# Value rows of tile 0 summed by VectorE, those of the other tiles in fours of slots, and a tenth ring place

## The reference

```
z   = x @ w_in                                   # q, k, v, GLU value, GLU gate
att = dilated sliding-window attention(q, k, v)  # 8 heads of 64
cv  = swish(LayerNorm(causal depthwise conv of the GLU output, 31 taps))
x1  = LayerNorm(ALPHA * x + concat(att, cv) @ w_out)
# PEER: 8 heads, each picks 16 of 16384 experts for each position
q   = x1 @ w_query
top 16 of both halves of the keys, then the best 16 of the 256 sums -> experts, gates
y_p = sum over the 128 chosen experts e:  gate_e * gelu(x1 . U[e]) * V[e]
y   = LayerNorm(ALPHA * x1 + y_p)
```

## Time and profile before

| | us |
|---|---|
| median of 3 runs (lowest to highest) | 4052.86 (4046.16 to 4052.99) |
| profiled execution | 4054.08 |
| its span | 4052.3 |
| VectorE busy | 2703.9 (67%) |
| TensorE matmuls busy | 2865.7 (71%) |
| GpSimd busy | 1203.4 (30%) |
| ScalarE busy | 682.6 (17%) |
| bytes moved by DMA | 1385.80 MB, mean 342 GB/s |

### The profile page before, as it was taken

The page is one execution under the profiler, slowest core; times in us unless marked ns, Lnnn a source line. Parts: engine busy times, 40 slices in busy tenths (PEclk is TensorE's granted clock), DMA queues, the critical chain, the costliest instruction groups (busy, mean ns, idle before and its releaser), DMA issues.

```text
span 4052.3 us, 41343 instructions
## 1 busy us (share of the span) xinstructions
PE 2865.7 (71%) x14768; PEld 1255.5 (31%) x14768; DVE 2703.9 (67%) x7412; ACT 682.6 (17%) x1484; POOL 1203.4 (30%) x1092
## 2 busy tenths in 40 slices
PE   6976554778567667666766876687677666779766
PEld 5422221334222313332332333233223332223311
DVE  4233343335586998699679868976997696445965
ACT  1200012210022013102310330132014101121000
POOL 0011111111144433433444344424333442223232
PEclk8987777889788888888888888879878988889989
DMA  9954468577689998998999899979988999999888
GB/s 334 345 202 155 151 225 290 206 277 291 226 328 408 411 366 326 422 413 345 372 419 400 330 395 419 394 290 416 414 355 325 421 408 391 415 417 365 335 329 349
DMA packets 217518, 1385.80 MB, mean 342 GB/s; under 512 B 27416, under 2 KB 38168, under 8 KB 66648
## 3 DMA queue, kind: packets, MB, share of 16 engines
q0 software_dynamic: 156672, 1140.92, 70.6%
q1 hardware_dynamic: 40384, 142.88, 9.8%
q10 hardware_dynamic: 20256, 99.35, 6.4%
HBM read 1369.94 MB, written 80.04 MB: 358 GB/s over the span
## 4 chain that ended last, share of the span: by engine, by line
PE 33%; DMA 29%; DVE 25%; issue 10%; POOL 2%; ACT 1%; DVEq 0%; ACTq 0%; POOLq 0%; SPq 0%
DMA t<-in_expert_uv,t 28%; PE psum L1367 20%; DVE t L1036 8%; PE psum L1214 4%; DVE t L1047 3%; PE psum L1256 2%; PE psum L1234 2%; POOL t L603 2%; DVE t L984 1%; DVE t L982 1%; DVE t L985 1%; DVE t L983 1%; PE psum L1245 1%; DVE t L927 1%; DVE t L981 1%
## 5 line engine op out<-in xcount | busy, mean ns | idle before, releaser
L1367 PE MATMUL psum<-t,t 64*64 64x512 f32 x5696 | 1627.2, 712 | 777.9 <-DVE t L1047 777.6
L603 POOL DMA_INDIRECT t<-in_expert_uv,t x1088 | 1203.2, 1106 | 2819.4 <-PE psum L1367 1403.2
L1036 DVE CUSTOM_DVE_ANT_0 t<-t,t 128x1024 f32<-128x1024 f32 x1088 | 1325.2, 1222 | 1039.0 <-DMA t<-in_expert_uv,t 1031.5
L1367 PEld LDWEIGHTS psum<-t,t 64*64 64x64 f32 x5696 | 415.9, 155 | 1746.1 <-DVE t L1047 983.1
L1363 PE MATMUL psum<-t,t 64*64 64x512 f32 x2496 | 760.4, 738 | 0.0
L754 ACT ACTIVATE t<-t 128x2 f32<-128x2 f32 x544 | 110.6, 203 | 2472.5 <-DVE t L1036 2465.6
L1047 DVE TENSOR_SCALAR t<-t,t,t 128x64 f32<-128x64 f32 x1088 | 294.0, 321 | 68.0 <-ACT t L754 59.1
L1324 PEld LDWEIGHTS psum<-t,t 128*128 128x128 f32 x2304 | 271.7, 197 | 54.0 <-issue 53.9
L1324 PE MATMUL psum<-t,t 128*128 128x128 f32 (+1 forms) x2304 | 281.8, 282 | 0.0
L1214 PE MATMUL psum<-t,t 128*128 128x128 f32 (+2 forms) x768 | 253.8, 489 | 8.2 <-DMA t<-in_xT 7.5
L903 DVE SCALAR_TENSOR_TENSOR t<-t,t,t 128x128 f32<-128x128 f32 x840 | 237.8, 344 | 0.0
(11 more groups left out here) (132 smaller groups left out, 1965.4 us busy)
## 6 DMA issues: line engine op xcount, KB each, us to landing
t<-in_wq_t ACTq DMA_DIRECT2D x63, 1024.0 KB
out<-in_cache_k_win SPq DMA_DIRECT2D x8, 4080.0 KB
out<-in_cache_v_win SPq DMA_DIRECT2D x8, 4080.0 KB
t<-in_w_in_t ACTq DMA_DIRECT2D x44, 512.0 KB, 5.1
t<-in_kc_t SPq DMA_DIRECT2D x8, 2560.0 KB
t<-in_vc_t SPq DMA_DIRECT2D x8, 2560.0 KB, 13.7
t<-in_expert_uv,t POOLq DMA_INDIRECT x1088
t<-in_w_v_t ACTq DMA_DIRECT2D x6, 1024.0 KB, 8.6
```

What stands on the lines that cost most here:

```text
L603: pool.indirect_dma_start(ring[:, r, :], None, I["expert_uv"], bass.IndirectOffsetOnAxis(ap=idn[t % 2][:, s:s + 1], axis=0)).then_inc(land ...
L1036: dve.tensor_tensor_reduce(out=ring[:, r, 0:D], in0=x1[t % 2][:, :], in1=ring[:, r, 0:D], scale=1.0, scalar=0.0, op0=ALU.mult, op1=ALU.add ...
L1367: last = pe.matmul(MAIN[t][half][NS * a:NS * a + NS, :], zt[NS * a:NS * a + NS, k % Z_RING, j, :], vv[NS * a:NS * a + NS, :], start=(p == ...
```

## The change

- Tile 0: no matmuls. `first_values` (DVE) multiplies two coefficients by their gates and then adds each V row, scaled, into two PSUM banks, one instruction of 128x1024 a slot. The new semaphore `v_done` counts them and releases ring places one at a time.
- Tiles 1 to 8: `gelu`, `weigh` and `values_quad` work on four slots. `weigh` is now two instructions: a product of four columns and one 128x256 product with both operands broadcast. `pv` counts fours. The lag of DVE and PE is one place, and DVE does the dot of a place before it weighs. `AUX_QUADS` are slots 12 to 119 (before 16 to 119).
- `RING` is 10; `wq0` and its load go, and every tile loads head 0's weights with head 1's.
- 48 early slots in place of 49, with gates of three heads in place of four.
- The 31 taps spread over 40 places, and `conv_rows` to `ln1_end` and `x1_transposes` come three to eight places later (the transposes of the attention keep theirs); the two output projections are two places apart in place of four, both `ln1_half` one place apart; `queries` and `query_copy` come two and one places later.

```diff
-RING, FIRST_RING = 9, 4
-Z_RING = 3
+RING, FIRST_RING = 10, 4
+Z_RING = 2
+TAP_SPAN = 40
-EARLY = ROUTE_STEP
-EARLY_GATES = (EARLY * (PH - 1) + TOP - 1) // TOP
+EARLY = 3 * TOP
+EARLY_GATES = EARLY // TOP
-AUX_PAIRS = range(8, PAIRS - 4)
+AUX_QUADS = range(3, QUADS - 2)
+def batch(t):
+    return 4 if t else 2
+            if (_s + 1) % batch(_t) == 0:
+                BATCH_PLACE.setdefault(place(_n, _q), []).append((_t, _s // batch(_t)))
+def tap_at(q):
+    return range(q * CK // TAP_SPAN, (q + 1) * CK // TAP_SPAN) if q < TAP_SPAN else range(0)
-        wq0 = at(o_l, [P, KD, 2 * KEYC])
-        zt = small([P, Z_RING, 2, NS])
+        zt = small([P, Z_RING, 4, NS])
+        first_sum = psum[:, 6 * 512:8 * 512]
-            sp.dma_start(wq0[:, :, :], I["wq_t"][0]).then_inc(wq0_in, 16)
...
# gather (POOL)
-                        pool.wait_ge(pv, pair(0, s - FIRST_RING) + 1)
+                        pool.wait_ge(v_done, s - FIRST_RING + 1)
-                        pool.wait_ge(pv, pair(1, k - RING) + 1)
+                        pool.wait_ge(pv, (k - RING) // 4 + 1)
# route_loads, query_copy (ACT)
-                for h in (1, 2):
+                for h in (0, 1):
-                if 1 <= h < PH - 2:
+                if h < PH - 2:
# DVE
-            def weigh(t, p):
-                k = PAIRS * t + p
-                dve.wait_ge(a_gelu, k + 1)
+            def weigh(t, c):
+                k = quad(t, c)
+                d4, g4 = dots[t % 2][:, 4 * c:4 * c + 4], gtn[t % 2][:, 4 * c:4 * c + 4]
+                dve.wait_ge(a_gelu, gelus(t, c) + 1)
+                step(dve.tensor_tensor(d4, d4, g4, ALU.mult))
                 if k >= Z_RING:
                     dve.wait_ge(pv, k - Z_RING + 1)
-                for j in range(2):
-                    s = 2 * p + j
-                    dve.tensor_scalar(zt[:, k % Z_RING, j, :], ident2[:, :], dots[t % 2][:, s:s + 1], gtn[t % 2][:, s:s + 1],
-                                      ALU.mult, ALU.mult).then_inc(zt_ready, 1)
+                dve.tensor_tensor(zt[:, k % Z_RING, :, :], ident2[:, :].unsqueeze(1).broadcast_to([P, 4, NS]),
+                                  d4.unsqueeze(2).broadcast_to([P, 4, NS]), ALU.mult).then_inc(zt_ready, 1)
+            def first_values(c):
+                d2 = dots[0][:, 2 * c:2 * c + 2]
+                dve.wait_ge(a_gelu, gelus(0, c) + 1)
+                step(dve.tensor_tensor(d2, d2, gtn[0][:, 2 * c:2 * c + 2], ALU.mult))
+                for s in (2 * c, 2 * c + 1):
+                    r, _ = spot(0, s)
+                    w_ = dots[0][:, s:s + 1]
+                    if s == 0:
+                        dve.tensor_scalar(first_sum, ring[:, r, D:ROW], w_, None, ALU.mult).then_inc(v_done, 1)
+                    else:
+                        dve.wait_ge(v_done, s)
+                        dve.scalar_tensor_tensor(first_sum, ring[:, r, D:ROW], w_, first_sum, ALU.mult, ALU.add).then_inc(v_done, 1)
-                        for t, p in pairs_at(n, q, 2):
-                            weigh(t, p)
                         for s in slots_at(n, q):
                             dot(max(n, 0), s)
+                        for t, c in batches_at(n, q, 1):
+                            if t:
+                                weigh(t, c)
+                            else:
+                                first_values(c)
-                if m and 4 * g + i < CK:
-                    taps(m, 4 * g + i)
+                for k in tap_at(4 * g + i) if m else ():
+                    taps(m, k)
-                if g in (12, 13) and i == 2:
-                    ln1_half(m, g - 12)
+                if g == 14 and i in (0, 1):
+                    ln1_half(m, i)
# PE
-                pe.wait_ge(zt_ready, 2 * (k + 1))
-                for half in range(2):
-                    for j in range(2):
+                pe.wait_ge(zt_ready, k + 1)
+                for two in range(2):
+                    for half in range(2):
+                        for j in (2 * two, 2 * two + 1):
-                if g in (11, 12):
-                    out_projection(m, g - 11)
+                if g == 13 and i in (1, 3):
+                    out_projection(m, i // 2)
-                        for t, p in pairs_at(n, 4 * g + i, 3):
-                            values_pair(t, p)
+                        for t, c in batches_at(n, 4 * g + i, 1):
+                            if t:
+                                values_quad(t, c)
```

More of the change, by code:

```diff
@@ L820, in front @@
                     weights_T(m, g - 1)
+                for h in range(PH):
+                    if g == QUERY_AT[h] and i == 3:
+                        query_copy(m, h)
+                        if h == 0:
+                            x1_rows(m)
                 if i != 2:
                     return
-                if g == 9:
+                if g == 11:
                     conv_std(m)
-                if g == 10:
+                if g == 12:
                     conv_swish(m)
@@ L844, in _ @@
                     for i in range(4):
-                        for t, p in pairs_at(n, 4 * g + i, 0):
-                            gelu(t, p)
+                        for t, c in batches_at(n, 4 * g + i, 0):
+                            gelu(t, c)
                         if m < PT:
@@ L1315, in queries @@
                     pe.wait_ge(x1T_ready, KD * (m + 1))
[L1317 to L1321, removed]
+                pe.wait_ge(wq_in[h % 2], 16 * (4 * m + h // 2 + 1))
+                w_ = wq[:, h % 2, :, :]
                 for side in range(2):
@@ L1339, in key_scores, with values_quad @@
                 last.then_inc(a_s, 1)
[L1341 to L1345, removed]
+            def values_quad(t, c):
+                k = quad(t, c)
+                w = slots(t) // 4
+                aux = t in AUX_TILES and c in AUX_QUADS
+                if c == 0:
                     if t == 1:
@@ L1351, in values_pair @@
                         pe.wait_ge(satt_T, 2 * NB)
[L1352 removed]
+                if aux and c == AUX_QUADS.start:
                     pe.wait_ge(res_done, t)
[L1354 to L1368 removed]
@@ new lines, in values_quad @@
+                pe.wait_ge(zt_ready, k + 1)
+                for two in range(2):
+                    for half in range(2):
+                        for j in (2 * two, 2 * two + 1):
+                            r, _ = spot(t, 4 * c + j)
+                            vv = ring[:, r, D + half * 512:D + (half + 1) * 512]
+                            if t == PT:
+                                last = pe.matmul(MAIN[t][half][0:NS, :], zt[:, k % Z_RING, j, :], vv, start=(c == 0 and j == 0), stop=(c == w - 1 and j == 3))
+                            elif aux and j % 2:
+                                for a in range(2):
+                                    last = pe.matmul(AUX[t][half][NS - NS * a:P - NS * a, :], zt[NS * a:NS * a + NS, k % Z_RING, j, :], vv[NS * a:NS * a + NS, :],
+                                                     start=(c == AUX_QUADS.start and j == 1), stop=(c == AUX_QUADS.stop - 1 and j == 3))
+                            else:
+                                for a in range(2):
+                                    last = pe.matmul(MAIN[t][half][NS * a:NS * a + NS, :], zt[NS * a:NS * a + NS, k % Z_RING, j, :], vv[NS * a:NS * a + NS, :],
+                                                     start=(c == 0 and j == 0), stop=(c == w - 1 and j == 3 and t not in AUX_TILES))
@@ L1472, in front @@
                             x1_rows(m)
+                    if g == QUERY_AT[h] + 1 and i == 1:
+                        key_scores(m, h)
+                if g == 13 and i in (1, 3):
+                    out_projection(m, i // 2)
+                if i != 1:
+                    return
+                if g == 10:
+                    att_transposes(m)
+                    conv_rows(m)
+                if g == 12:
+                    conv_back(m)
+                if g == 15:
+                    x1_transposes(m)
             for n in range(-1, TILES + 1):
```

90 lines of the change are left out of this document (33 added, 57 removed).

## The result

| | us |
|---|---|
| after, median of 4 runs (lowest to highest) | 3930.71 (3928.28 to 3934.43) |
| before, median of 4 runs of the same sitting | 4052.93 |
| ratio, 95% interval | 0.9703 (0.9686 to 0.9720) |
| span of the profiled execution after | 3932.6 |

The account below looks back on a forecast made before the run. Tile 0 was taken as bound by a loop through all engines, tiles 1 to 6 by VectorE and DMA by turns; 120 + 108 + 39 - 2 = 265 us saved from 4052.3 gave 3788, range 3700 to 3890.

Parts of the forecast that it names:

- 120 + 108 saved: Tile 0 without matmuls: 120 us saved in stage -1 (245 for 365), 108 in stage 0 (440 for 548).
- The 15 us to the first landing: Start of stage -1: 15 us until the first gather lands, counted in the 245 us forecast for that stage.
- The 9 and 46 us added for projections and copies: Tile 0: 9 us added to stage -1 for copies or projections, 46 to stage 0 for ScalarE's projection waits.
- I take 5 us a tile for both together: Tiles 1 to 6: ring turning in fours plus later `ln1_half` cost 5 us a tile, between 0 and 18.
- 2.5 to 4: Tiles 1 to 8, at a four's release: gathers DMA still keeps, against about 4.5 with pairs; tenth place returns one.
- my signs of being wrong: Sum over 1.4 us, gelu waits in tile 0 over 50 us, or DMA share under 0.93 in tiles 1 to 6.
- -10 and -4 for VectorE's relief: Tiles 1 to 6: fewer early taps and cheaper weigh save 10 us in a tile's first part, 4 in its third.
- +2.6 for the weights: Loading head 0's weights, 1 MB for each tile, costs 2.6 us a tile where DMA bounds, with no stall.
- +3.65 at the end: End of tile 8: the last four takes twice the last pair's 3.65 us, so 3.65 us is lost.
- Fours starve the ring: Rival, chance 0.13: tiles 1 to 6 lose 10 us each in place of 6.5 saved, giving 3887 us.
- The last rival, slower than before: Rival, chance 0.03: release of fours in tiles 1 to 8 costs 2 us each, about 4307; break-even 1.3 us.
- GpSimd is held by the sums: Rival, chance 0.04: tile 0's sums hold back gathers, each round 1.2 us longer, 77 in all, giving 3865.

Follow-up runs that it names:

- front_old: The changed kernel with the front (taps, convolution, output projection, LayerNorm, queries) back at the places of the kernel before: 3930.85 us, ratio to before 0.9688.
- r10_both: The changed kernel with pairs in place of fours, apart from small differences (early slots, `zt` buffers, AUX start): 3734.11 us, ratio to before 0.9223.
- ring9: The changed kernel with nine ring places in place of ten: 4129.46 us, ratio to before 1.0200.
- split2: The changed kernel with ring places released in twos and the second half of a four's matmuls two places later on TensorE: 3791.64 us, ratio 0.9373.
- t0_ring10: The kernel before with tile 0's sums by VectorE, head 0's weights loaded every tile and ten ring places, still pairs and old front: 3751.07 us, ratio 0.9264.
- split2_front_old: split2 with the front's old places: 3800.02 us, ratio to before 0.9379.
- t0_nowq: The kernel before with tile 0's sums by VectorE and head 0's weights loaded every tile, nine ring places, pairs, old front: 3795.68 us, ratio 0.9394.
- r10_front_new: t0_ring10 with the front's new places: 3720.32 us, ratio to before 0.9184.

## Why the prediction was wrong

**Tile 0: right, and a little low.** 120 + 108 saved was the sum, 139 + 124 came (364.7 to 226.1, 547.9 to 423.8; the start was 2 us later). A round was 9.0 where I had 9.2. The 15 us to the first landing was a misreading: that piece of the chain begins with the third gather, at 193.44. The first dot starts 8.6 us after the first gather in the kernel before, and 8.1 after it in the changed one:

```profile
199.41 1.22 DVE L1036 CUSTOM_DVE_ANT_0 t<-t,t 128x1024 f32<-128x1024 f32 x1 [8.66 <-DMA t<-in_expert_uv,t]
```

```profile
201.16 1.23 DVE L1050 CUSTOM_DVE_ANT_0 t<-t,t 128x1024 f32<-128x1024 f32 x1 [8.21 <-DMA t<-in_expert_uv,t]
```

That is 7 of the 19 us by which stage -1 came out shorter than my 245. The sum's price was 1.22 and is 1.289 in this row, 9 us more over tile 0:

```profile
L1076 DVE SCALAR_TENSOR_TENSOR psum<-t,t,psum 128x1024 f32<-128x1024 f32 x127 | 163.7, 1289 | 4.9 <-DVE t L1068 0.4
```

The 9 and 46 us added for projections and copies were too much: stage 0 took 424 us, 30 above my floor of 394. Its DMA share is 0.89, so the DMA engines were busy for 377 of the 424.

**The step that failed** is "I take 5 us a tile for both together". With it tiles 1 to 6 were to gain 6.5 us each (the four terms add up to 6.4); they lost 17.6 each on average. The second half of that term was right: `ln1_half` waits 4 us a tile, and `front_old` shows that this costs nothing.

```profile
DVE t L981 <- PE psum L1325: 32.8, 8, 11.4
```

The first half, the ring in fours, was mis-sized: against `r10_both` tiles 1 to 6 lose 2365 - 2222 = 143 us, 24 a tile, more than my upper end of 18 for both. Three things were wrong in it. First, a four with AUX was taken as 3.8 us, twice a pair at full clock; it takes 6.3 in the round above. Second, I had computed "2.5 to 4" gathers left ("The tenth place gives back one") and priced that at next to nothing. The medians from issue to landing say how many were really under way; these are `ring9`, the changed kernel, `split2` and `t0_ring10`:

```profile
t<-in_expert_uv,t POOLq DMA_INDIRECT x1088, 9.7
```

```profile
t<-in_expert_uv,t POOLq DMA_INDIRECT x1088, 10.1
```

```profile
t<-in_expert_uv,t POOLq DMA_INDIRECT x1088, 10.8
```

```profile
t<-in_expert_uv,t POOLq DMA_INDIRECT x1088, 12.5
```

Divided by the time from gather to gather in tiles 1 to 6 (2517, 2365, 2248 and 2237 us for 768), that makes about 3.0, 3.3, 3.7 and 4.3 gathers under way, an estimate from these rows, at DMA shares of 0.87, 0.92, 0.96 and 0.96. The medians are over all tiles, and a reserve at the release is not an average, so this is rough; but it is 3.3 where I had 3.5 to 5 with the tenth place, and the DMA share of 0.92 shows that the DMA engines run dry for part of the time. Third, the sum took an average where the places differ. I had 7.3 us for a four without AUX and let it stand among the others; at the border of two tiles it takes 9.9, and 98 of the 143 us are lost there. And the sum had no term for the order of ScalarE and TensorE: beside the attention the four, the value matmuls, `normalise`, the exp and the gelu make a round of 13.57 us for four slots, where four landings at 2.6 take 10.4. The cover that I named, VectorE's idle 37% in the middle of a tile, reaches neither. And one of my signs of being wrong came: the DMA share of tiles 1 to 6 is under 0.93. The others did not: the sum is under 1.4 us, and the waits of `first_values` for the gelu in tile 0 are 13 us in all.

**-10 and -4 for VectorE's relief**: VectorE is 65 us less busy in tiles 1 to 6, but the stretch is longer. With fours the relief of VectorE by the taps buys nothing (`front_old`, `split2_front_old`: no difference); with pairs the front's new places, the spread taps among them, buy 31 us, where I had 8 us of taps in each of six tiles. That the late ring is why they buy nothing with undivided fours fits the traces; why they still buy nothing in `split2`, with its DMA share of 0.96, stays open.

**+2.6 for the weights**: of the right size as far as `t0_nowq` can tell. **+3.65 at the end**: the last four takes 8.59 us where the last pair took 3.65, so +4.9, and tile 8 lost 21 in all. TensorE's four takes 7.1 us there, and after a pause of 4.4 us it starts at a slower rate (two matmuls in 1.97 us), as does the last one:

```profile
3814.54 7.08 PE L1391 MATMUL psum<-t,t 128*64 128x512 f32 x16 [1.48 <-DVE t L1061]
...
3821.90 1.49 POOL L615 DMA_INDIRECT t<-in_expert_uv,t  x1 [3.77 <-PE psum L1391]
...
3826.03 1.97 PE L1391 MATMUL psum<-t,t 128*64 128x512 f32 x2 [4.41 <-DVE t L1061]
...
3913.55 8.59 PE L1391 MATMUL psum<-t,t 128*64 128x512 f32 x16 [4.49 <-DVE t L1061]
```

**The rivals.** "Fours starve the ring" is what happened: it gave 10 lost a tile and 3887; 17.6 were lost on average in tiles 1 to 6, and tiles 7 and 8 lost another 34, which it did not count. Its price was too low, and it had only an average ring in it, not the fours without AUX or the round through gelu and attention. The last rival, slower than before, was the same mechanism: with nine places it happened (1.0200). Its break-even was reckoned wrongly: 265 already holds the 39, and from its own 3827 it is (4053 - 3827) / 240 = 0.94 us for each four, not 1.3. By the 195 us between the changed kernel and `r10_both` a four cost 0.8. "GpSimd is held by the sums" fell: in the round of tile 0 the gather at 308.09 starts while the second sum runs, and takes 0.94 us.

## What to carry to other kernels

Where gathers run through a ring, count the ring's reserve at the worst moment: gathers still in flight when a release comes, against the landing time under load. Batching the work that frees places coarsens the release; release inside the batch as each part is done. Batching also makes one long piece of work on an engine that others wait for: follow the round through every engine, without the DMA too, and let the engine go between the parts. The second helped here only together with the first. When a change has several parts, time the part with the clear mechanism alone: here tile 0's sums gave 6.8%, and the rest took back more than half of it. The fastest kernel keeps tile 0's sums, the tenth place and the front's new places, and has pairs.

## What the runs showed of the hardware

A dot with both operands in SBUF holds a gather's issue back, a sum with one operand in PSUM doesn't. In tile 0 of the changed kernel the gather issued 0.07 us into a dot takes 1.97 us, the one issued during a sum 0.94 (308.09 in the round above); the timeline of both engines just behind it:

```profile
309.35 1.23 DVE L1050 CUSTOM_DVE_ANT_0 t<-t,t 128x1024 f32<-128x1024 f32 x1 [0.20 <-DMA t<-in_expert_uv,t]
309.42 1.97 POOL L615 DMA_INDIRECT t<-in_expert_uv,t  x1 [0.39 <-DVE psum L1076]
```

The Trainium skill says so of the dot ("SBUF — State Buffer", section "SBUF: two separate sides"): the pair of ports that VectorE and GpSimd share is locked for a VectorE instruction with two SBUF inputs, against a GpSimd instruction that reads SBUF.

The granted clock goes with the idle time: in tiles 1 to 6 of `ring9`, the changed kernel, `split2` and `r10_front_new` it is 0.79, 0.81, 0.84 and 0.85, as the DMA share goes 0.87, 0.92, 0.96 and 0.97. In the round of tile 4 the matmuls after the waits take 1.12 us and the last of the four 0.59. So a starved ring seems to make the matmuls slower that should release it; no run held the one fixed to show it apart.
